# Expert scores interleaved with the query products, and 20 instead of 28 early expert tiles

## What is computed

```python
def _peer(h, w_q, k1, k2, u_tab, v_tab):            # 16384 experts, 8 heads, top 16
    q = (h @ w_q).reshape(b, l, PEER_HEADS, 2, PEER_HALF)
    s1 = jnp.einsum('blhc,hnc->blhn', q[..., 0, :], k1)
    s2 = jnp.einsum('blhc,hnc->blhn', q[..., 1, :], k2)
    v1, i1 = lax.top_k(s1, PEER_TOPK)
    v2, i2 = lax.top_k(s2, PEER_TOPK)
    cand_s = (v1[..., :, None] + v2[..., None, :]).reshape(b, l, PEER_HEADS, PEER_TOPK * PEER_TOPK)
    cand_i = (i1[..., :, None] * PEER_N_KEYS + i2[..., None, :]).reshape(...)
    top_s, pos = lax.top_k(cand_s, PEER_TOPK)
    idx = jnp.take_along_axis(cand_i, pos, axis=-1)
    g = jax.nn.softmax(top_s, axis=-1)
    # per token: sum over its 128 experts of g * gelu(u_tab[idx] . h) * v_tab[idx]
```

## Time and profile before

| | |
|---|---|
| Timed runs | 3069.15, 3076.06, 3077.77 us; median 3076.06 |
| Profiled execution | 3069.55 us, span 3067.8 us |
| TensorE busy | 2913.7 us, 95% of the span |
| VectorE busy | 2009.2 us, 65% |
| ScalarE busy | 1096.6 us, 36% |
| Mean granted TensorE clock | 0.97 |

### The profile page before, as it was taken

The page is one execution under the profiler, slowest core; times in us unless marked ns, Lnnn a source line. Parts: engine busy times, 40 slices in busy tenths (PEclk is TensorE's granted clock), DMA queues, the critical chain, the costliest instruction groups (busy, mean ns, idle before and its releaser), DMA issues.

```text
span 3067.8 us, 50224 instructions
## 1 busy us (share of the span) xinstructions
PE 2913.7 (95%) x19440; PEld 2476.8 (81%) x19440; DVE 2009.2 (65%) x3760; ACT 1096.6 (36%) x1771; POOL 83.8 (3%) x88
## 2 busy tenths in 40 slices
PE   8998999998999989999999999988998999999997
PEld 6785997785997548888999998865888899999985
DVE  3765883765884333998666666773299866666677
ACT  2423552332552211133444444430113344444443
POOL 0022000022000000000000000000000000000000
PEclk9899999899999999999999999988999999999999
DMA  5204873203882124522555555643352255545563
GB/s 195 91 17 165 327 303 127 109 17 136 319 326 97 69 69 158 186 90 97 181 188 178 189 180 192 244 169 136 137 192 83 92 189 178 188 181 183 186 244 148
DMA packets 77557, 502.53 MB, mean 164 GB/s; under 512 B 9072, under 2 KB 9456, under 8 KB 20592
## 3 DMA queue, kind: packets, MB, share of 16 engines
q1 hardware_dynamic: 71520, 481.92, 43.3%
q10 hardware_dynamic: 5904, 18.71, 1.7%
HBM read 488.02 MB, written 12.58 MB: 163 GB/s over the span
## 4 chain that ended last, share of the span: by engine, by line
PE 85%; DVE 11%; issue 1%; ACT 1%; DMA 1%; POOL 1%; DVEq 0%; ACTq 0%; SPq 0%; POOLq 0%
PE bank L813 22%; PE bank L825 21%; PE bank L858 8%; PE bank L520 4%; PE bank L1959 4%; PE bank L1913 4%; PE bank L1968 4%; PE bank L651 3%; PE bank L1776 2%; PE bank L718 1%; PE bank L507 1%; PE bank L1796 1%; DVE sb L2184 1%; DVE sb L2177 1%; DVE sb L2178 1%
## 5 line engine op out<-in xcount | busy, mean ns | idle before, releaser
L825 PE MATMUL bank<-peer_pass_high,peer_pass_hidden 128*128 128x512 f32 x1344 | 452.4, 397 | 0.0
L813 PE MATMUL bank<-peer_pass_high 128*128 128x256 f32 x1344 | 383.3, 285 | 13.8 <-DVE ring_r L920 13.8
L813 PE MATMUL bank<-peer_pass_high,ring_r 128*128 128x256 f32 x1344 | 385.7, 287 | 0.0
L813 PE MATMUL bank<-hT_r,peer_pass_high 128*128 128x256 f32 x1344 | 381.1, 284 | 0.0
L920 DVE TENSOR_TENSOR ring_r<-ring,peer_pass_high 128x1024 fp32r<-128x1024 f32 x168 | 205.9, 1225 | 196.1 <-ACT peer_pass_high L1502 196.1
L825 PEld LDWEIGHTS bank<-peer_pass_high,peer_pass_hidden 128*128 128x128 f32 x1344 | 253.9, 189 | 53.7
L813 PEld LDWEIGHTS bank<-peer_pass_high 128*128 128x128 f32 x1344 | 257.4, 191 | 22.7 <-issue 14.8
L1502 ACT ACTIVATE peer_pass_high<-ring 128x1024 fp32r<-128x1024 f32 x168 | 178.3, 1061 | 270.0 <-DMA ring<-in_experts 269.2
L825 PE MATMUL bank<-ring_r,peer_pass_hidden 128*128 128x512 f32 x672 | 267.4, 398 | 0.0
L813 PEld LDWEIGHTS bank<-hT_r,peer_pass_high 128*128 128x128 f32 x1344 | 257.6, 192 | 7.0
L813 PEld LDWEIGHTS bank<-peer_pass_high,ring_r 128*128 128x128 f32 x1344 | 257.1, 191 | 0.0
(11 more groups left out here) (345 smaller groups left out, 5517.3 us busy)
## 6 DMA issues: line engine op xcount, KB each, us to landing
ring<-in_experts SPq DMA_DIRECT2D x256, 1024.0 KB, 4.8
ring<-in_w SPq DMA_DIRECT2D x139, 1024.0 KB, 4.8
sb<-in_w_mod SPq DMA_DIRECT2D x48, 1024.0 KB, 6.7
spill<-sb ACTq DMA_DIRECT2D x22, 512.0 KB, 6.6
sb<-spill SPq DMA_DIRECT2D x44, 256.0 KB, 5.0
sb<-in_ln ACTq DMA_DIRECT2D x8, 512.0 KB, 4.9
sb<-in_post ACTq DMA_DIRECT2D x4, 512.0 KB, 5.1
sb<-in_ctx SPq DMA_DIRECT2D x2, 1024.0 KB, 13.4
```

Of the source, the lines that this page charges most:

```text
L813: m = pe.matmul(ps[u][:, 0:S], w, h[:, kt, :], start=(kt, i) == (0, 0), stop=(kt, i) == (KT - 1, 2))
L825: m = pe.matmul(ps[4 + 2 * tb + half][:, :], g[:, t], w, start=False, stop=False, skip_group_check=True)
```

## The change

- The keys get a buffer of their own (`k.keys`) and a transfer on ScalarE's queue (`act_keys`): for layer 0 at the end of the attention, for layer 1 at the start of the pooling stage, ahead of inv_count. The segment of query weights has 8 slots instead of 9.
- TensorE: scores of head h - 1, for both halves of the tokens, directly after the query product of head h; the last head's after the first early tile. All query products are copied by ScalarE.
- VectorE selects in five batches over both token halves: heads 0; 1; 2, 3; 4, 5; 6, 7. Gates and indices are formed for four heads at a time, after the third and the fifth batch, with instructions of half the size, twice as many.
- ScalarE: the first exponential ahead of the first early tile and of the last head's scores, the second ahead of early tile 14.
- EARLY_SELECT goes from 28 to 20, so 92 instead of 84 tiles are in the pass and 36 instead of 44 are early.

```diff
-MLA_SLOTS, QK_SLOTS, EXPERTS, POOL_SLOTS = 12, 9, 128, 9
-EARLY_SELECT, EARLY_BUILD = 28, 16
+MLA_SLOTS, QK_SLOTS, EXPERTS, POOL_SLOTS = 12, 8, 128, 9
+EARLY_SELECT, EARLY_BUILD = 20, 16
-GATES_BEFORE = (11, 26)
+GATES_BEFORE = 14
+KEY_SLOTS = (12 + QK_SLOTS, 30 + QK_SLOTS)
+BATCHES = ((0, 1), (1, 2), (2, 4), (4, 6), (6, 8))
...
 def peer_jobs():
     j = [(("xt", i), both(i)) for i in range(4)]
-    j += [(("q", i), both(i)) for i in range(8)]
-    j += [(("s", i), "act") for i in range(8)]
-    j += [(("eu", t), "act") for t in range(EARLY_SELECT)]
+    j += [(("q", 0), "act")]
+    for h in range(1, PH):
+        j += [(("q", h), "act"), (("s", h - 1), "act")]
+    j += [(("eu", 0), "act"), (("s", PH - 1), "act")]
+    j += [(("eu", t), "act") for t in range(1, EARLY_SELECT)]
...
+    def score(h):
+        J.evac(pe, ("q", h), l)
+        b = J.give(pe, ("s", h), l)
+        for tb in range(TB):
+            for a in range(2):
+                hh = 2 * h + a
+                m = pe.matmul(ps[b][:, (2 * tb + a) * P:(2 * tb + a + 1) * P], k.qT[:, hh, tb * P:(tb + 1) * P],
+                              k.keys[:, hh * P:(hh + 1) * P], start=True, stop=True)
+                rel.pay(m)
...
+    query(0)
+    pe.wait_ge(k.keys_loaded, 16 * (l + 1))
+    for h in range(1, PH):
+        query(h)
+        score(h - 1)
+    early_up(0)
+    score(PH - 1)
+    for t in range(1, EARLY_SELECT):
+        early_up(t)
...
+def dve_select(k, v, sd, h0, h1):
+
+    both = [(tb, hh) for tb in range(TB) for hh in range(2 * h0, 2 * h1)]
+    dve_top16(k, v, sd, [(k.s[:, tb, hh, :], k.s2[:, tb, hh - 2 * h0, :], k.val[:, tb, hh, :], k.ix[:, tb, hh, :]) for tb, hh in both])
+    sd.done(v.tensor_copy(k.ixf[:, :, 2 * h0:2 * h1, :], k.ix[:, :, 2 * h0:2 * h1, :]))
+    for tb in range(TB):
+        val = k.val[:, tb, :, :].rearrange("p (h a) k -> p h a k", a=2)[:, h0:h1, :, :]
+        cand = k.cand[:, tb, 0:h1 - h0, :].rearrange("p h (a b) -> p h a b", b=TOPK)
+        sd.done(v.tensor_tensor(cand, bc(val[:, :, 0, :].unsqueeze(3), h1 - h0, TOPK, TOPK),
+                                bc(val[:, :, 1, :].unsqueeze(2), h1 - h0, TOPK, TOPK), ALU.add))
+    sd.settle()
+    both = [(tb, h) for tb in range(TB) for h in range(h0, h1)]
+    dve_top16(k, v, sd, [(k.cand[:, tb, h - h0, :], k.cand2[:, tb, h - h0, :], k.top[:, tb, h, :], k.pos[:, tb, h, :]) for tb, h in both])
...
+    for a, pos in enumerate((k.posa, k.posb)):
+        for tb in range(TB):
+            sd.done(v.tensor_tensor(eq(tb), bc(k.c["iota"][:, 0:TOPK].unsqueeze(1).unsqueeze(1), n, TOPK, TOPK),
+                                    bc(pos[:, tb, hs, :].unsqueeze(3), n, TOPK, TOPK), ALU.is_equal))
+        for tb in range(TB):
+            ixf = k.ixf[:, tb, :, :].rearrange("p (h a) k -> p h a k", a=2)[:, hs, a, :]
+            sd.settle(1 - tb)
+            sd.done(v.tensor_tensor(eq(tb), eq(tb), bc(ixf.unsqueeze(2), n, TOPK, TOPK), ALU.mult))
+        for tb in range(TB):
+            sd.settle(1 - tb)
+            sd.done(v.tensor_reduce(k.sel[:, tb, a, hs, :], eq(tb), AX.X, ALU.add))
+        sd.settle()
...
+    for h0, h1 in BATCHES:
+        J.evac(v, ("s", h1 - 1), l)
+        dve_select(k, v, sd, h0, h1)
+        if h1 % (PH // 2) == 0:
+            dve_gates(k, v, sd, l, h1 * 2 // PH - 1)
...
+def act_keys(k, a, l):
+
+    a.dma_start(k.keys, k.dram["w2"][KEY_SLOTS[l]]).then_inc(k.keys_loaded, 16)
...
+    query(0)
+    for h in range(1, PH):
+        query(h)
+        score(h - 1)
+    gates(0)
+    early_up(0)
+    score(PH - 1)
+    for t in range(1, EARLY_SELECT):
+        if t == GATES_BEFORE:
+            gates(1)
+        early_up(t)
...
     a.wait_ge(k.x2_done.sem, 2)
+    act_keys(k, a, 1)
```

More of the change, by code:

```diff
@@ L1729, in plan_memory2 @@
     k.s = r.take(TB, HH, NK)
[L1730 to L1736, removed]
+    k.s2 = r.take(TB, 4, NK)
+    k.val, k.ixf = r.take(TB, HH, TOPK), r.take(TB, HH, TOPK)
+    k.ix = r.take(TB, HH, TOPK).bitcast(U32)
+    k.cand, k.cand2 = (r.take(TB, 2, TOPK * TOPK) for _ in range(2))
+    k.top, k.posa, k.posb = (r.take(TB, PH, TOPK) for _ in range(3))
+    k.pos, k.pa_, k.pb_ = (r.take(TB, PH, TOPK).bitcast(U32) for _ in range(3))
+    k.keys = r.take(SLOT)
+    k.eq = r.take(TB, PH // 2, TOPK * TOPK)
+    k.gsum = r.take(TB, PH // 2)
     k.sel = r.take(TB, 3, PH, TOPK)
@@ L1905, in pe_peer, with query @@
     J.evac(pe, ("xt", 3), l)
-    seg = f"qk{l}"
     rel = Release(k)
-    for i in range(8):
-        w = slot(k, pe, seg, i)
-        b = J.give(pe, ("q", i), l)
+    def query(h):
+        w = slot(k, pe, f"qk{l}", h)
+        b = J.give(pe, ("q", h), l)
         for kk in range(2):
@@ L1917, in pe_peer, with early_up @@
         rel.owe()
[L1918 to L1927, removed]
+    def score(h):
[7 more added lines that the diff above has]
+                rel.pay(m)
         m.then_inc(J.filled, 1)
-    rel.owe()
-    for t in range(EARLY_SELECT):
+    def early_up(t):
         w = slot(k, pe, f"early{l}", t // 2)
@@ L2168, in dve_mla, with dve_top16 @@
     dve_post_norm(k, v, sd, J, 0)
-def dve_top16(k, v, sd, src, spare, val, idx, n):
-    for h in range(n):
-        sd.done(v.max(val[:, h, 0:8], src(h)))
+def dve_top16(k, v, sd, rows):
+    for src, spare, val, idx in rows:
+        sd.done(v.max(val[:, 0:8], src))
     sd.settle()
-    for h in range(n):
-        sd.done(v.match_replace(spare(h), val[:, h, 0:8], src(h), NEG))
-        sd.done(v.max_index(idx[:, h, 0:8], val[:, h, 0:8], src(h)))
+    for src, spare, val, idx in rows:
+        sd.done(v.match_replace(spare, val[:, 0:8], src, NEG))
+        sd.done(v.max_index(idx[:, 0:8], val[:, 0:8], src))
@@ L2179, in dve_top16 @@
     sd.settle()
-    for h in range(n):
-        sd.done(v.max(val[:, h, 8:16], spare(h)))
+    for src, spare, val, idx in rows:
+        sd.done(v.max(val[:, 8:16], spare))
     sd.settle()
-    for h in range(n):
-        sd.done(v.max_index(idx[:, h, 8:16], val[:, h, 8:16], spare(h)))
+    for src, spare, val, idx in rows:
+        sd.done(v.max_index(idx[:, 8:16], val[:, 8:16], spare))
     sd.settle()
+def dve_select(k, v, sd, h0, h1):
[10 more added lines that the diff above has]
+    dve_top16(k, v, sd, [(k.cand[:, tb, h - h0, :], k.cand2[:, tb, h - h0, :], k.top[:, tb, h, :], k.pos[:, tb, h, :]) for tb, h in both])
@@ new lines, in dve_gates @@
+def dve_gates(k, v, sd, l, part):
+    n = PH // 2
+    hs = slice(part * n, part * n + n)
+    top = k.top[:, :, hs, :]
+    v.tensor_tensor(k.sel[:, :, 2, hs, :], top, bc(top[:, :, :, 0:1], TB, n, TOPK), ALU.subtract).then_inc(k.gate2_arg.sem, 1)
+    sd.done(v.tensor_scalar(k.pa_[:, :, hs, :], k.pos[:, :, hs, :], 4, None, ALU.logical_shift_right))
+    sd.link(v.tensor_scalar(k.pb_[:, :, hs, :], k.pos[:, :, hs, :], 15, None, ALU.bitwise_and))
+    sd.done(v.tensor_copy(k.posa[:, :, hs, :], k.pa_[:, :, hs, :]))
+    sd.link(v.tensor_copy(k.posb[:, :, hs, :], k.pb_[:, :, hs, :]))
+    eq = lambda tb: k.eq[:, tb, :, :].rearrange("p h (a b) -> p h a b", b=TOPK)
+    for a, pos in enumerate((k.posa, k.posb)):
[10 more added lines that the diff above has]
+        sd.settle()
+    v.wait_ge(k.gate2_exp.sem, k.gate2_exp.at(part + 1, l))
+    sd.link(v.tensor_reduce(k.gsum[:, :, :], k.sel[:, :, 2, hs, :], AX.X, ALU.add))
+    sd.link(v.reciprocal(k.gsum[:, :, :], k.gsum[:, :, :]))
+    v.tensor_tensor(k.sel[:, :, 2, hs, :], k.sel[:, :, 2, hs, :], bc(k.gsum[:, :, :].unsqueeze(3), TB, n, TOPK), ALU.mult)\
+     .then_inc(k.sel_ready.sem, 1)
@@ L2191, in dve_peer @@
     dve_affine(k, v, sd, J, 2 * l, l)
[L2192 to L2222, removed]
@@ L2347, in act_peer, with query, score, gates @@
     mod_evac(k, a, J, "act", "xt", lambda kt: k.hT[:, kt, :], k.hshift[:, 2 * l, :], k.hscale[:, 2 * l, :], l)
[L2348 to L2361, removed]
+    def query(h):
+        b = J.take(a, "act", ("q", h), l)
+        a.activation(k.qT[:, 2 * h:2 * h + 2, :], shaped(k.psum[b][:, :], 2, S), ACT.Copy).then_inc(J.read["act"], 1)
+    def score(h):
+        b = J.take(a, "act", ("s", h), l)
+        a.activation(k.s[:, :, 2 * h:2 * h + 2, :], shaped(k.psum[b][:, :], TB, 2, NK), ACT.Copy).then_inc(J.read["act"], 1)
+    def gates(part):
+        hs = slice(part * PH // 2, (part + 1) * PH // 2)
+        a.wait_ge(k.gate2_arg.sem, k.gate2_arg.at(part + 1, l))
+        a.activation(k.sel[:, :, 2, hs, :], k.sel[:, :, 2, hs, :], ACT.Exp).then_inc(k.gate2_exp.sem, 1)
+    def early_up(t):
         b = J.take(a, "act", ("eu", t), l)
@@ L2577, in build @@
         k.ln_loaded = sem("ln_loaded")
+        k.keys_loaded = sem("keys_loaded")
         k.zp_cleared = sem("zp_cleared")
```

1 line of the change is left out of this document (added).

## The result

| | before | changed |
|---|---|---|
| Timed | 3076.06 us (3069.15 to 3081.36, 5 runs) | 3054.03 us (3052.20 to 3054.76, 5 runs) |
| Profiled execution | 3069.55 us, span 3067.8 | 3054.28 us, span 3052.5 |
| Ratio, changed / before | | 0.9931 (0.9917 to 0.9945) |

The kernel is 22.0 us faster by the medians, 0.69%. The forecast was 3045.5 us, a gain of 27.3; the measured time is 8.5 us above it and within the range.

What follows compares the result with a forecast made beforehand. TensorE, busy 95% of the span, bounds the kernel, with VectorE's selection setting the end of its stage. Gains of 9.1 + 2.0 + 12.0 + 4.2 = 27.3 us from a middle base of 3072.8 gave 3045.5 us, range 3036 to 3058.

Steps and rivals of the forecast that it cites:

- Part 1: TensorE, early tiles: each tile moved to the pass saves 0.57 us; 8 tiles in 2 layers save 9.1 us.
- Part 2: TensorE before the first score: the 0.99 us wait for VectorE's query copy goes in both layers, saving 2.0 us.
- Part 3: Selection on VectorE ends 2.9 us before TensorE's filler, so the 5.98 and 5.97 us waits go: 12.0 us.
- Part 4: ScalarE's two exponentials, ahead of early tiles and head 7's scores: any waits are covered, cost nothing.
- Part 5: Table build after the selection: its first groups run at the 2.4 GHz level, saving 4.2 us of 4.3 lost.
- rival B: Clock stays low at the table build, all else as forecast: gain 23.1 us, 3049.7 us; chance 0.10.
- Part 6: Keys' transfer moves to ScalarE's queue: costs nothing; in layer 1 inv_count still lands with 5 us of cover.
- the clock's part: The 4.2 us that the table build was to gain from a full clock, within the 27.3 us sum.
- two bases 6.5 us apart: Starting times for the sum: the profiled execution gives 3042.3 us, the timed median 3048.8; the middle, 3045.5, was taken.
- rival A: Selection on VectorE ends after the filler, 1 to 5 idle us a layer: 3048 to 3060 us; chance 0.18.

Runs made afterwards that it cites:

- The moved tile: Changed kernel with its twentieth early tile moved behind the selection's transposes and ScalarE's spill wait moved to table group 32: 3041.00 us, ratio to before 0.9879.
- second set of runs: Changed kernel timed again without edit: 3051.49 us, ratio 0.9917, beside the kernel before at 3078.42 us.

## Why the prediction was right, and where it was off

- **Part 1, the tiles: right.** Forecast was 0.57 us a tile. From 28 to 20 tiles in the new order, the stages of the undisturbed layer gave 4.4 us for 8 tiles, 0.55 each. (The prediction counts records where it says 64 score matmuls and 16 longer ones in a tile: a float32 matmul leaves two, so it is 32 and 8. The prices don't change.)
- **Part 2, the wait before the scores: right.** It is gone in both layers. Scores start 13.9 us after the first query product (1165.56 - 1151.67); the 14.9 that I gave as their start is where the first ones end.
- **Part 3, the cover of the selection: right, and with it the sum.** Forecast was that VectorE starts 15.65 us after the first query product (measured 15.68), that one head takes 10.4 us (10.34), two heads 19.3 (1190.75 to 1210.00, 19.25), the gates of four heads 16.0 (1210.00 to 1226.11, 16.1), and that it is done 2.9 us before TensorE (2.4). VectorE's whole way from the first query product to its last gate instruction was forecast at 129.15 us and took 129.11; the missing 0.5 is on TensorE's side, which came to the transposes after 131.5 us instead of 132.0. The gap of 5.98 and 5.97 us went wholly. The count of 20 is bracketed by two runs: 16 tiles bring 11.31 us of idle time a layer, 28 cost 12.0 us in all. Between them no run decides; by the rows a nineteenth tile left out would save 0.57 us and bring back about 1.1 of idle time (3.46 - 2.4), an estimate. The Trainium skill's warning against small tiles, which the prediction quotes (VectorE: DVE Perf Modes, "The TRN2 errata — SBUF-src ops pay a fixed extra latency per instruction"), did not decide. The trace agrees that small instructions pay more per element, 0.420 us for 256 elements against 1.222 for 1024, but the price was the one that the rows of before gave, and the cover held. The 58 cycles (60 ns) that the prediction takes from that section's table are too few for it; the section's own figure for float32 tensor_tensor, 151 cycles, gives an estimate of 0.157 us, which is what the rows show (0.16).
- **Part 4, ScalarE: right, with one wait that I had not seen.** The argument of the first exponential was there at 1210.2 and ScalarE came at 1213.94; the second one waited 0.54 us, which the cover that was forecast for it took in. But the last spill is now issued at 1283.83, directly before the table build, and ScalarE may not write the table until it has landed:

```profile
1290.74 0.60 ACT L2429 ACTIVATE sb<-bank 128x512 f32<-128x512 f32 x1 [5.66 <-DMA spill<-sb]
```

  This copy ends at 1291.3, and TensorE wants the bank back at its fifth group, at 1295.7, so four banks cover it with 4.4 us to spare. I had cost the spills at nothing without naming this cover.
- **Part 5, the clock: wrong.** This is the step that failed. I let the slow start of the table build go with the 6 us gap, 4.2 us in all. The tables took 246.4 us in both layers before and 245.6 after: 0.8 us. The gap that is left, 0.82 us of transposes and 2.94 idle, is enough for the granted clock to be 0.54 and 0.51 behind it. Even the 0.8 can't be credited to the change with any safety: with 28 tiles in the new order, behind the same gap, the table stages took 124.0 and 122.7 us, a spread of 1.3. The reason that I gave, that the smaller part of the gap is left, was no reason; rival B had it right. The sign that I had set for B, a first table group of over 2.5 us, would have missed it: the group alone took 1.57 us (1286.97 to 1288.54), and only the pair of group and tile quarter, 3.28 against 1.76 at full clock, shows the loss. The moved tile shows what the term was worth when the gap is filled: tables of 242.1 us, 3.5 less.
- **Part 6, the keys: right.** Transfer and first use in layer 1, keys and inv_count:

```profile
sb<-in_w ACTq DMA_DIRECT2D x1, 1024.0 KB, 4.7
sb<-in_const ACTq DMA_DIRECT2D x1, 512.0 KB, 5.6
...
2053.42 0.45 ACTq L2452 DMA_DIRECT2D sb<-in_const  x1
...
2068.68 0.69 DVE L2307 TENSOR_TENSOR sb<-sb 128x512 f32<-128x512 f32 x1
```

  inv_count lands 1.9 us later than it did after its issue (5.6 against 3.7 us), at 2059.0, the two side by side rather than in turn, and is used 9.7 us after that. The forecast had the two in turn and 5 us of cover; there was more.
- **The sum and the base.** Without the clock's part the forecast was 23.1 us. The profiles give 24.5 between the same two instructions: 23.1, 0.8 of clock and 0.2 a layer at the transposes, the rest too small to place. The timed medians give 22.0 in the first set of runs and 26.9 in the second set of runs. Of the 8.5 us by which 3054.0 lies above 3045.5, the clock term is 3.4 (4.2 - 0.8). The remaining 5 are not in the changed stages but in the base: the first query product started between 1142.0 and 1157.7 us in ten profiles, and I had taken the middle between two bases 6.5 us apart without seeing that the base itself moves by more than the term in doubt. So the total alone decides nothing here: 3054.0 is nearer to rival B (3049.7) than to the forecast, and it lies in the middle of rival A's 3048 to 3060. That the idle time before the transposes is gone rules A out, and the table stages tell B from the forecast. What decides the clock in the first block was not tried.

## What to carry to other kernels

When one engine selects while another needs filler, give the selector its inputs piece by piece from the first one on, and only then cut the filler: the order matters (the cut without the interleaving made the stages 52.6 us longer than before, while the interleaving without the cut still gave 12.5 of the 24.5 us). Size the filler by adding up both engines' chains from their last common event; row by row, that gave the margin within 0.5 us on a chain of 90. And count a gap on TensorE twice, for its length and for the clock behind it: the single tile moved into a gap of 2.94 us made a kernel that beats both, at 3041.0 us, some 6 to 7 us of it by the stages.

## What was not expected of the hardware

- A gap of 2.94 us behind 0.82 us of transposes brought the granted clock to 0.54 and 0.51 in the 3.4 us after it, where the 5.98 + 1.54 + 2.38 us of before had brought it to 0.54 and 0.50. Idle 0.93 us, then transposes, then a float32 tile left it at 1.00.
- The clock behind the same gap cost different amounts: with 28 tiles in the new order layer 0's first window was at 0.50 and the second at 0.64, its table stage 124.0 us against 122.8 in the changed kernel.
- Two executions of one kernel started the same stage up to 3.7 us apart, and ten profiles with the same first block 15.7 us apart. The same matmuls kept TensorE busy for 1067.9 to 1083.4 us before it, and the time in which it was not busy stayed within 2 us. An effect under some 5 us is better read from stage lengths than from the total.
